# A two-block network on one core: where the norm's sums are taken, how the first scan begins and ends, and which columns the levels of the second scan multiply

## The reference, cut to what matters

```python
# block 1
xn = rmsnorm(h, norm_mix); u = xn @ w_in            # q, k, v, o, gates
h  = h + mlstm_mixer(...)                           # forward and backward scan, 4 heads
h  = h + sqrelu_mlp(...); h = h + gate * (p @ ple_w)
# mLSTM step per chunk of 128 tokens and direction
d   = exp(log_d - m_t)                              # decays inside the chunk
s   = (q k^T) * d
num = s @ v + inter * (q @ C^T)
h   = num / max(|den|, exp(-m_t))
C   = decay * C + (w * v)^T k                       # state for the next chunk
# block 2
p   = (rms_norm(x) * (1 + scale) + shift) @ w_in
y_a = rwkv7_scan(...)        # state = state*w + sa b + v k, 8 heads of 64
y_b = sparse attention (top 256 keys per query)
x   = x + gate * (merged @ w_o)
```

## Time and profile before

| | |
|---|---|
| median of 3 runs | 2606.39 us (2603.94 to 2608.79) |
| the profiled execution's own time | 2603.65 us |
| its span | 2601.9 us |
| PE matmul busy | 2485.8 us (96%) |
| PE weight load busy | 2026.5 us (78%) |
| DVE | 1376.1 us (53%) |
| ACT | 855.4 us (33%) |
| POOL | 982.1 us (38%) |
| mean granted TensorE clock | 0.99 of full speed |

### The profile page before, as it was taken

How to read it: one execution, slowest core, us unless ns; L and a number is a source line. 1 busy time by engine, 2 the same in 40 slices (tenths; PEclk the granted TensorE clock), 3 DMA queues, 4 the chain that set the end, 5 groups by cost and what they waited for, 6 DMA issues and landing times. The chain is left out here.

```text
span 2601.9 us, 41079 instructions
## 1 busy us (share of the span) xinstructions
PE 2485.8 (96%) x17441; PEld 2026.5 (78%) x17441; DVE 1376.1 (53%) x2007; ACT 855.4 (33%) x1410; POOL 982.1 (38%) x521
## 2 busy tenths in 40 slices
PE   7998999999999999999999989999997998898998
PEld 5887778888888888888877658778785777786786
DVE  6112543253253221222676499999994665566842
ACT  3213553321121110123453365544525542223231
POOL 3212414444243342344563216546523102221774
PEclk9999999999999999999999999999999999999999
DMA  3112303122222211112324303234233002102423
GB/s 135 42 50 89 122 27 111 49 74 84 84 84 83 72 50 45 49 49 66 97 74 164 95 20 135 77 108 140 77 106 126 19 15 92 37 4 88 166 75 112
DMA packets 82086, 207.68 MB, mean 80 GB/s; under 512 B 8393, under 2 KB 21745, under 8 KB 81905
## 3 DMA queue, kind: packets, MB, share of 16 engines
q1 hardware_dynamic: 74992, 192.48, 22.3%
q10 hardware_dynamic: 6912, 12.59, 1.3%
HBM read 170.81 MB, written 35.27 MB: 79 GB/s over the span
## 5 line engine op out<-in xcount | busy, mean ns | idle before, releaser
L332 PE MATMUL ps<-region_rounded,weights_hi_by_slot 128*128 128x512 f32 x2432 | 962.9, 396 | 25.1 <-DVE region_rounded L610 14.0
L334 PE MATMUL ps<-region_rounded,weights_lo_in_place 128*128 128x512 f32 x2432 | 949.2, 390 | 0.0
L333 PE MATMUL ps<-region_rounded,weights_hi_by_slot 128*128 128x512 f32 x2432 | 949.1, 390 | 0.0
L326 POOL TENSOR_TENSOR weights_lo_in_place<-wbuf,weights_hi_by_slot 128x1024 fp32r<-128x1024 f32 x194 | 484.1, 2498 | 691.9 <-ACT weights_hi_by_slot L322 691.5
L332 PEld LDWEIGHTS ps<-region_rounded,weights_hi_by_slot 128*128 128x128 f32 x2432 | 458.4, 189 | 129.5 <-issue 32.7
L334 PEld LDWEIGHTS ps<-region_rounded,weights_lo_in_place 128*128 128x128 f32 x2432 | 458.1, 188 | 96.4
L333 PEld LDWEIGHTS ps<-region_rounded,weights_hi_by_slot 128*128 128x128 f32 x2432 | 458.5, 189 | 95.4 <-issue 3.6
L322 ACT CAST weights_hi_by_slot<-wbuf 128x1024 fp32r<-128x1024 f32 x194 | 201.9, 1043 | 382.5 <-DMA wbuf<-w_mlp 216.0
L2136 DVE MAX8 gcols<-region 128x8 f32<-128x384 f32 (+5 forms) x192 | 171.6, 894 | 6.6
L2138 DVE MATCH_REPLACE8 region<-gcols,region 128x384 f32<-128x384 f32 (+5 forms) x192 | 168.2, 876 | 0.0
L1421 POOL TENSOR_TENSOR region_rounded<-region,region_rounded 128x512 fp32r<-128x512 f32 x64 | 83.0, 1297 | 215.2 <-DVE region_rounded L1576 215.2
(11 more groups left out here) (348 smaller groups left out, 3366.4 us busy)
## 6 DMA issues: line engine op xcount, KB each, us to landing
wbuf<-w_mlp SPq DMA_DIRECT2D x64, 512.0 KB, 3.6
wbuf<-w_hn SPq DMA_DIRECT2D x37, 512.0 KB, 4.1
wbuf<-w_in SPq DMA_DIRECT2D x25, 512.0 KB, 3.7
region<-xT SPq DMA_DIRECT2D x24, 512.0 KB, 6.7
xtra<-w_ada SPq DMA_DIRECT2D x32, 384.0 KB, 4.2
scratch_hn_out<-tmp ACTq DMA_DIRECT2D x48, 256.0 KB, 3.8
region<-scratch_hn_out SPq DMA_DIRECT2D x24, 512.0 KB, 7.8
wbuf<-w_att SPq DMA_DIRECT2D x20, 512.0 KB, 3.7
```

The costliest lines, as they stand in the source:

```text
L326: self.nc.gpsimd.tensor_tensor(self.m.lo4[:, n % SLOTS, :], self.m.raw4[:, n % SLOTS, :], self.m.hi4[:, n % SLOTS, :].bitcast(F32), ALU.su ...
L332: nc.tensor.matmul(out, m.hi4[:, s, w], m.rounded(hi + k, half(hf)), start=(k == 0), stop=False)
L333: nc.tensor.matmul(out, m.hi4[:, s, w], m.rounded(lo + k, half(hf)), start=False, stop=False)
L334: return nc.tensor.matmul(out, m.lo4[:, s, w], m.rounded(hi + k, half(hf)), start=False, stop=(k == KT - 1))
```

## The change

Three places.

1. **Front.** The two matmuls with ones stand inside the first half product of the third unit, ahead of its second and third tile (k = 1, 2), instead of behind the first and the second half product. ACT makes the high parts of units 4 and 5 behind the roots.
2. **First scan.** POOL's masks and ACT's decays of units 0 and 1 move to the end of the front. The tail's four weight loads go one by one behind the row loads of u = 5, 7, 9, 11; its high and low parts of two units go to the end of ACT's and POOL's work. The units of the last step (14 and 15) make no weighted values, no states and no state updates. ACT makes the output gate's first two high parts (k = 0, 1) at its end, and DVE their low parts ahead of the last unit's normalizers.
3. **Second scan.** Each level product has 32 moving columns, those that grow at this level, packed in the bank; the number of matmuls stays. The mask is one of 128x128 per half; the growth is one operation of 128x128 for the rows and one for the columns of each half. On PE the second half's q1 of level l - 1 is interleaved with y1 of level l, and the first half's q1 with the second half's q0. y1 has a buffer of its own for each level, cleared once by POOL.

```diff
+def scan_mask(nc, m, u):
+    d = SCAN_UNITS[u][0]
+    mask = m.const("mask_bwd" if d else "mask_fwd").unsqueeze(1).to_broadcast([P, MH, L])
+    nc.gpsimd.tensor_tensor(m.tmp[:, 4 + d, :].rearrange("p (h t) -> p h t", h=MH), m.tmp[:, d, :].rearrange("p (h t) -> p h t", h=MH),
+                            mask, ALU.add).then_inc(m.masked, 1)
...
+def scan_decays(nc, m, act, u):
+    d, c, _ = SCAN_UNITS[u]
+    r = scan_row(d, c)
+    act.wait_ge(m.masked, u + 1)
+    for h in range(MH):
+        a = m.tmp[:, 4 + d, h * L:(h + 1) * L]
+        ins = nc.scalar.activation(a, a, ACT.Exp, bias=m.gcols[:, 0, r + h:r + h + 1], scale=-1.0)
+    ins.then_inc(m.decay_ready, 1)
...
+            def squares_summed(k):
+                if k == 1:
+                    pe.wait_ge(consts_loaded, 16)
+                if 1 <= k < 3:
+                    pe.wait_ge(all_added, k)
+                    nc.tensor.matmul(m.ps[:, 5 + k, :], m.const("ones"), even[:, half(k - 1)], start=True, stop=True
+                                     ).then_inc(summed, 1)
...
-                    st.half_product(pe, n, bank(n, hf), hf, XF, XR, taken, j - BANKS + 1)
-                    if n == 2:
-                        if hf == 0:
-                            pe.wait_ge(consts_loaded, 16)
-                        pe.wait_ge(all_added, hf + 1)
-                        nc.tensor.matmul(m.ps[:, 6 + hf, :], m.const("ones"), even[:, half(hf)], start=True, stop=True
-                                         ).then_inc(summed, 1)
+                    st.half_product(pe, n, bank(n, hf), hf, XF, XR, taken, j - BANKS + 1, squares_summed if j == 4 else None)
...
-            for n in range(2, 6):
+            for n in range(2, 4):
...
-                if 6 <= n + 2 < FRONT:
+                if n + 2 < FRONT:
                     st.hi(act, n + 2)
...
+                if n == FRONT - 2:
+                    act.wait_ge(cols_copied, 1)
+                    for u in range(2):
+                        scan_decays(nc, m, act, u)
...
+            pool.wait_ge(cols_copied, 1)
+            for u in range(2):
+                pool.wait_ge(m.rows_loaded[0][u], 16)
+                scan_mask(nc, m, u)
...
-            for n in range(SLOTS):
-                m.tail.load(sp, n, m.d["w_in"][FRONT + n])
             for u in range(2, n_units + 2):
...
+                n = u - 5
+                if n >= 0 and n % 2 == 0 and n < 2 * SLOTS:
+                    m.tail.load(sp, n // 2, m.d["w_in"][FRONT + n // 2])
...
             for u, (d, c, s) in enumerate(units):
-                pool.wait_ge(rows_loaded[0][d], 16 * (u // 2 + 1))
                 if u >= 2:
+                    pool.wait_ge(rows_loaded[0][d], 16 * (u // 2 + 1))
...
+                    scan_mask(nc, m, u)
...
-                if u == n_units - 3:
-                    m.tail.lo(pool, 0)
-                    m.tail.lo(pool, 1)
+            m.tail.lo(pool, 0)
+            m.tail.lo(pool, 1)
...
-            decays(0)
             for u, (d, c, s) in enumerate(units):
-                if u + 1 < n_units:
-                    decays(u + 1)
-                if u >= 2:
+                if 2 <= u + 1 < n_units:
+                    scan_decays(nc, m, act, u + 1)
+                if u >= 2 and s < NC - 1:
                     act.wait_ge(state_ready, MH * (u - 1))
-                for h in range(MH):
-                    r = scan_row(d, c) + h
-                    ins = nc.scalar.mul(wv[d][:, h, :], m.values[:, c, h, :], m.gcols[:, 1, r:r + 1])
-                ins.then_inc(wv_ready, 1)
+                if s < NC - 1:
+                    for h in range(MH):
+                        r = scan_row(d, c) + h
+                        ins = nc.scalar.mul(wv[d][:, h, :], m.values[:, c, h, :], m.gcols[:, 1, r:r + 1])
+                    ins.then_inc(wv_ready, 1)
                 if 1 <= u <= first_half:
                     take_heads(u - 1)
-                if u == n_units - 4:
-                    m.tail.hi(act, 0)
-                    m.tail.hi(act, 1)
+            for n in range(2):
+                m.tail.hi(act, n)
+            act.wait_ge(x_again, 16 * KT)
+            act.wait_ge(scores_ready, n_units)
+            act.wait_ge(qi_ready, n_units - 2)
+            for k in range(OG_EARLY):
+                nc.scalar.mul(m.rounded(OX + k), m.chunk(ORAW + k), m.par("norm_mix", k)).then_inc(m.o_hi, 1)
...
+                if s < NC - 1:
+                    pe.wait_ge(wv_ready, u + 1)
+                    for h in range(3):
+                        state(u, h)
                 if u + 2 < n_units:
                     scores(u + 2)
-                state(u, 3)
+                if s < NC - 1:
+                    state(u, 3)
...
-            for u in range(n_units):
+            for u, (d, c, s) in enumerate(units):
+                if u == n_units - 1:
+                    for k in range(OG_EARLY):
+                        rest_of_gate_input(nc, m, dve, k)
                 normalizers(u)
                 if u >= first_half:
                     add_heads(u, (0, 1))
-                update_states(u, (0, 1, 2))
+                if s < NC - 1:
+                    update_states(u, (0, 1, 2))
                 if u >= first_half:
                     add_heads(u, (2, 3))
-                update_states(u, (3,))
+                if s < NC - 1:
+                    update_states(u, (3,))
...
+def rest_of_gate_input(nc, m, dve, k):
+    dve.wait_ge(m.o_hi, k + 1)
+    nc.vector.scalar_tensor_tensor(m.rounded(ORAW + k), m.chunk(ORAW + k), m.par("norm_mix", k),
+                                   m.rounded(OX + k).bitcast(F32), ALU.mult, ALU.subtract).then_inc(m.o_lo, 1)
...
+            for k in range(OG_EARLY, KT):
...
+            for k in range(OG_EARLY, KT):
+                rest_of_gate_input(nc, m, dve, k)
...
+    inv, invt = t[:, 0:512], t[:, 512:1024]
+    g_s, ra_tok, x0 = t[:, 1536:2048], t[:, 2048:2560], t[:, 2816:3328]
+    y1s = [None, m.xtra[:, 0:512], m.xtra[:, 512:1024], m.xtra[:, 1024:1536], t[:, 1024:1536], t[:, 3328:3840]]
+    def blocks(ap, l, q):
+        return ap.rearrange("r (n two s) -> r n two s", two=2, s=1 << l)[:, :, q, :]
...
+    def y1_bank(i, l, hh):
+        return rows_bank(i, hh) if l % 2 else 3 - rows_bank(i, hh)
+    def q0_bank(i, l, hh):
+        return 3 - y1_bank(i, l, hh)
+    def q1_bank(i, l, hh):
+        return y1_bank(i, l, hh) if l < LAST else 3 - rows_bank(i, hh)
...
+            def y1_product(i, l, hh, p, par):
+                r = tile64(par)
+                return nc.tensor.matmul(m.ps[tile64(par ^ hh), y1_bank(i, l, hh), half_cell(p)],
+                                        mats_s[r, i % 2, par, hh, p, 64:128], blocks(hx(inv, p, hh)[r], l, 0),
+                                        start=True, stop=True)
+            def q0_product(i, l, hh, p, par):
+                o = tile64(par ^ hh)
+                return nc.tensor.matmul(m.ps[tile64(par), q0_bank(i, l, hh), half_cell(p)], hx(invt, p, hh)[o],
+                                        blocks(hx(y1s[l], p, hh)[o], l, 0), start=True, stop=True)
+            def q1_product(i, l, hh, p, par):
+                o = tile64(par ^ hh)
+                return nc.tensor.matmul(m.ps[o, q1_bank(i, l, hh), half_cell(p)], hx(y1s[l], p, hh)[o],
+                                        blocks(hx(invt, p, hh)[o], l, 1), start=True, stop=True)
...
+                if l == 1:
+                    pe.wait_ge(first_rows, 2 * i + 1)
+                else:
+                    pe.wait_ge(rows_grown, rows_count(i, l - 1, 0))
+                for p, par in groups:
+                    last = y1_product(i, l, 0, p, par)
+                last.then_inc(y1, 1)
+                if l == 1:
+                    pe.wait_ge(first_rows, 2 * i + 2)
+                else:
+                    pe.wait_ge(rows_grown, rows_count(i, l - 1, 1))
+                for p, par in groups:
+                    last = y1_product(i, l, 1, p, par)
+                    if l > 1:
+                        before = q1_product(i, l - 1, 1, p, par)
+                last.then_inc(y1, 1)
+                if l > 1:
+                    before.then_inc(q1, 1)
+                n = 2 * (LAST * i + l - 1)
+                pe.wait_ge(y1_masked, n + 1)
+                if l == 1:
+                    pe.wait_ge(invt_ready, i + 1)
+                    pe.wait_ge(tok_copied, 5 * (i + 1))
+                else:
+                    pe.wait_ge(cols_grown, cols_count(i, l - 1, 0))
+                if l == LAST:
+                    for hh in range(2):
+                        if hh:
+                            pe.wait_ge(y1_masked, n + 2)
+                            pe.wait_ge(cols_grown, cols_count(i, l - 1, 1))
+                        for p, par in groups:
+                            last = q1_product(i, l, hh, p, par)
+                        last.then_inc(q1, 1)
+                    return
+                for p, par in groups:
+                    last = q0_product(i, l, 0, p, par)
```

(73 more changed lines are left out.)

77 lines of the change are left out of this document (15 added, 62 removed).

## The result

The changed kernel takes **2582.95 us** (median of 4 runs, 2581.97 to 2586.19) against 2607.59 before (4 runs); the ratio is 0.9906, 95% interval 0.989 to 0.9922. That is faster by 24.6 us where 46.9 were forecast, and it lies above the range of 2544 to 2577.

A forecast was written before the change was run, and what follows sets the result against it. PE, busy for 96% of 2601.9 us, was taken as the bound. Terms of 6.8 + 5.0 + 10.0 + 25.0 = 46.8 us off 2603.65 gave 2556.9, and 2559.5 us as median; range 2544 to 2577.

The forecast's parts named there:

- The front (-6.8): Front: PE's stall of 4.85 us on the gate product goes, and 1.95 us of low clock behind it.
- The first scan's start (-5.0): First scan's start: without weight loads ahead, rows land earlier and unit 2's mask starts at 226.5 instead of 231.53.
- so the whole of 5.0 moves: First scan's first half: masks, decays and probabilities set the pace, so unit 2's earlier mask brings all 5.0 us.
- The first scan's end (-10.0): First scan's end and tail's start: 5.2 + 1.3 + 1.6 + 2.7 - 0.8 = 10.0 us from waits, clock and dropped work.
- The term of the early gate inputs: Tail's start: first matmul 2.7 us earlier, less 0.8 for DVE's low parts ahead of unit 15's normalizers.
- The second scan: Second scan: shorter levels give 3.1 us a pair, 3.8 in the first, less 0.5 for POOL's clearing; -25.0 us.
- the ring: Second scan's middle level: y1, mask, q products, growth, next y1 in turn, from 3.15 us to about 2.15.
- The sign named for being wrong: Wrong if the second scan shortens by under 15 or over 35 us, or another stage moves by 2.
- The clock there is 1.00: Second scan: the granted clock, read as full in the profile before, was assumed full for the new levels.
- rival 4: Second scan: levels ask so little of the array that the clock stays at 1.2 GHz; 2651.5 us for all pairs, chance 0.05.
- The price of 11.5 a pair: Second scan: the low clock costs 11.5 us in a new pair of some 23 us, PE on the path half the time.
- Rival 3: Second scan: the clock falls to 1.2 GHz in two pairs, giving 2582.5 us; chance 0.05.

The follow-up runs named there:

- run 10: The changed kernel with the tail's four weight loads back ahead of all rows of the first scan: 2589.95 us, one execution.
- run 4: The changed kernel with the tail's four weight loads later, behind the rows of units 10 to 13: 2586.89 us.
- Run 8: The changed kernel without the two early parts of the output gate's input, all eight made at the tail's start: 2587.94 us.
- Runs 3, 5 and 6: In this order the kernels cols64, spread64 and spread32: 2578.82, 2575.27 and 2586.84 us.
- spread32: The changed kernel (32 columns) with SP's loads of the second scan spread over the pairs: 2586.84 us.
- spread64: The changed kernel with 64 moving columns in the level products and SP's loads of the second scan spread over the pairs: 2575.27 us.
- cols64: The changed kernel with all 64 moving columns in each level product, new order and small DVE operations kept: 2578.82 us.
- spread_old: The changed kernel's front and first scan, the second scan's levels as before the change, its loads spread over the pairs: 2583.23 us.
- q1_quarter: spread64 with three quarters of the q1 products of levels 1 to 4 left out, so the output is another: 2557.0 us.

## Why the prediction was wrong where it was

**The front (-6.8): right.** -6.4 in the pair of traces; over the fourteen kernels with the changed front the mean is 201.8 against 208.6 in the two without, -6.8. Both parts came: the stall and the low clock behind it.

**The first scan's start (-5.0): right in its mechanism, the size was some 3.5.** Unit 2's mask moved by 5.3 as worked out (3.15 behind the issue, forecast 3.4). The step that failed is "so the whole of 5.0 moves": from unit 2's reciprocal to unit 8's the changed kernels take 42.0 to 43.4 us, for 40.9 and 41.9 in the two with the old first scan and 41.2 in run 10, so one to two us are given back in the first half. Run 10 prices the move at some 3.5; in run 4 the loads at their new places are not what gives it back. What sets that pace no run shows.

**The first scan's end (-10.0): right.** From unit 8's reciprocal to the tail's first matmul 54.6 became 44.9: -9.7. The term of the early gate inputs was 2.7 - 0.8 = 1.9. Run 8 finds 1.6 at the tail's first matmul: the gain is smaller than 2.7, and the cost of 0.8 doesn't show. The other terms of this sum were not taken apart.

**The second scan (-25.0, measured -3.2): the sum was wrong, the ring nearly right.** Its prices were met or nearly: 32 columns cost what 64 cost to 0.06 a level, DVE 0.285, the level 2.20 for 2.15, the pair 2.6 less instead of 3.1, mainly because level 5, counted as nothing, takes 0.34 more. The sign named for being wrong, a second scan shorter by under 15 us, came up. Two steps failed.

First, **the clock**. "The clock there is 1.00" was carried over to the new levels; as rival 4 the fall had 0.05, at all eight pairs. It fell in four, to 0.71 to 0.92. Runs 3, 5 and 6 show what the 32 columns do: that edit saves 0.06 a level, keeps the clock down for longer once it has fallen, and takes 11.6 us (spread32 against spread64; 2.8 on the stage, the changed kernel against cols64). My argument against rival 4 was the number of matmuls; it is not what counts, since spread32 has as many as spread64. The price of 11.5 a pair was too high, though: spread32's third pair took 31.1 at 0.74 against 27.0 at 1.00, so 4.1 for half of a pair at the low level. Rival 3, the low clock in two pairs, gave 2582.5, and 2582.95 was measured; that is luck, since four pairs were low in part, each at well under its price, and the holes made up the rest.

Second, **PE's own instructions**, which no step of the prediction had. I took the ring (PE, DVE, PE) as the only bound of a level and looked for the next one on DVE. It was the supply of instructions: a level asks for the same 192 records in 2.2 us instead of 3.15. At full clock the holes take 10 us more (14.0 in spread64 against 4.2 in spread_old); in the changed kernel it is 8 (11.9 against 3.8). By their order in time they also start the falls of the clock (run 3), so the two failures seem to hang together. The trace before had it in view: a hole of 1.7 in its fourth pair, and 55 blocks at 3.9 us apart.

By the runs at full clock the second scan's gain is 6.9 us with its holes (224.7 to 217.8), and with 32 columns the low clock takes part or all of it back. The Trainium skill ("TensorE: Matmul & The Clock Gate", section Back-to-back issue gap) has in its table of cycles one value of about 60 for all of 1 to 64 moving columns. This case agrees with that: 2.20 us a level with 32 columns, 2.26 with 64.

**The version to take** is the change with one edit less: its front, first scan and order of levels, but all 64 columns, take 2578.8, and with the loads spread 2575.3. Shown is that spread64 beats spread32 and spread_old (the intervals 0.9867 to 0.9897 against 0.9913 to 0.9938 and 0.9899 to 0.9926 are apart). From the changed kernel's 0.989 to 0.9922 neither of the two is clear, as the intervals overlap.

## What to carry to other kernels

Before cutting the columns of small matmuls, look whether a matmul's price goes by its columns at all; where it doesn't, the cut saves next to nothing, and here it cost the clock. When a loop of many small instructions gets shorter, divide its instructions by its new length and compare that with the fastest pace of the instruction blocks in the trace, as with any other engine. And read "issue" in the waits of before: here it was not zero (3.8 us), and every version with faster levels but q1_quarter made it more.

## What the runs showed that I had not expected

PE's instruction blocks of 16 KB never start nearer than 3.2 us to each other, and the holes of this stage stand where a block ends: 2.3 us of them at 67 matmul and load records a us in a middle level, 9.4 at 75, 14.0 at 85. The granted clock over the stage is 0.98 to 1.00 with 64 columns in all kinds of products (leaving out the runs with added waits), 1.00 with 64 in two of three, and 0.86 to 0.92 with 32 in all, and then not at the same pairs in every kernel. And a wait on a semaphore that is already up is far from free on PE: 640 of them cost 12 to 20 us.
